# Adding the expert gates into a zeroed DRAM scratch by indexed accumulating transfers, head by head, in place of one-hot products

## The chip, the cores and the metric

The kernel runs on one core of a Trainium2 chip. The metric is the device time of one execution in microseconds. PE is the matrix engine, DVE is VectorE, ACT is ScalarE, POOL is GpSimd; "PEld" is PE's weight load. SP issues the weight stream. A "q" behind a name is the engine's queue for DMA issues.

## What is computed

Two transformer blocks on 256 tokens of width 2048 in float32. The part that matters is the expert layer of the first block (`peer`):

```python
q = (t @ wq).reshape(T, 8, 2, 128)
s1 = einsum('thd,hnd->thn', q[:, :, 0], k1)      # 128 key scores per head and half
s2 = einsum('thd,hnd->thn', q[:, :, 1], k2)
v1, i1 = top_k(s1, 16)
v2, i2 = top_k(s2, 16)
cand = v1[..., :, None] + v2[..., None, :]       # 256 pairs
sc, pos = top_k(cand.reshape(T, 8, 256), 16)
idx = ...                                         # i1 * 128 + i2 of the 16 best pairs
g = softmax(sc)
act = gelu(einsum('thkd,td->thk', u[idx], t))
out = einsum('thk,thkd->td', g * act, v[idx])
```

There are 128 x 128 = 16384 experts; a token picks 8 heads x 16 of them.

## The kernel before

**How the layer is made dense.** For the first G = 48 tokens the kernel gathers the rows of the picked experts. For the other TD = 208 tokens it computes all experts: in eight rounds r, each of 2048 experts, a product u_r (16 feature units), gelu, a multiplication by the gates, and a product e_r (16 units). The gates of a token are a 128 x 128 matrix (second key by first key), zero but for the picked pairs, where they hold the sum of the softmax values. A round needs the gates of 16 first keys; they lie in DRAM (`gates_d`) and come in four loads of four first keys into `gbuf` (`load_gates(r, g)`, on POOL's queue).

**The weight stream.** Every product takes its weights from one stream of 1 MB units. SP loads unit k into `raw[k % 4]`. ACT writes its rounded high part into `split` (`hi`, line 713), DVE the rest (`lo`, line 1163), and PE multiplies high and low parts: 48 matmuls of 208 columns in a unit of u0 or u1 (lines 1996 to 1998). `ahead(u)` on ACT and DVE prepares the unit three behind u; from `NEAR0` on it is two behind, with the low part in `split` too, so that the load of the next unit need not wait for PE. The order of the stream around the change is wq (16 units), u0, u1, e0, e1, u2, e2 and so on.

**The order around the change, as written out by hand.** During wq, PE adds the key scores of head h in step `KEYS_AT`, ACT copies them to `s_sb`, and DVE searches the best 16 in two passes of eight (`best8`, lines 1515 to 1522: maximum, its index, its replacement), first of four key rows and then, after `sums` (line 1537), of two rows of pairs. Searches of two heads are interleaved, and a split (`ahead`, `fill`) stands between the pieces. This reaches into u0. Then, for all heads at once, DVE turns positions into keys (`differ`, lines 1586 and 1593), ACT takes the exponentials between u0's units, DVE divides by the sums. Picks lie in `picked`, transposed by PE into `pickT`.

**The gates in u1.** Tokens go in 52 groups of four. For each, DVE writes a one-hot tile of the second keys (`pick_b`, line 1619) and four of the first keys times the gate (`pick_a`, line 1624), PE multiplies them (`gate_group`, line 2341) at up to five places inside a u1 unit, ACT copies the bank to `stage` (line 950), and after four groups ACT's queue writes 1 MB to `gates_d` (line 954). The gates of the first eight first keys also go to `gbuf` directly (line 957). POOL meanwhile issues 36 small DMAs for the gathered tokens' indices, gates and scales (lines 628 to 630).

**Behind it.** DVE multiplies u0's result `act0` by the gates and splits it for e0 in four groups `gated0(g)` (lines 1642, 1654, 1657). e0's first unit needs all 16 tiles. During e0 DVE alternates `accumulate(0, k)`, `ahead` and `gated1(k)`, which does the same for u1's result and e1. Later rounds use `gate_hidden`. The gathers for the first 48 tokens (line 639, 96 of them) start behind e0.

Of the kernel before, what the change touches and what calls it, by code (L numbers as in the profile page):

```python
# [15 lines left out]
F32 = mybir.dt.float32  # L16
# [25 lines left out]
TBLOCK, TBLOCKS = 16, TD // 16  # L42
# [40 lines left out]
for _name, _n in [("ident", P), ("tri", P), ("ones", P), ("ntri", P), ("gt", P), ("flip", P),  # L83
                  ("mask", 2 * P), ("iota", P), ("sel", G)]:
    CONSTS[_name] = (_c, _c + _n)
    _c += _n
# [41 lines left out]
def build(nc, x_in, mem_in, stream, cols_in, consts_in, rows_in, wide_in, wdtf_in, keys_in,  # L128
          rel_in, onehot_in, u_rows, v_rows, out):
    ctx = ExitStack()  # L130
    with ctx:
# [89 lines left out]
        cand = at("cand", [P, 2, TT, 256], F32, work_at + 24576)  # L221
        differ = at("differ", [P, PICKS, TOPK], U32, work_at + 24576)
        pick_a = at("pick_a", [P, 8, P], F32, work_at + 24576)
        pick_b = at("pick_b", [P, 8, P], F32, work_at + 28672)
        gbuf = at("gbuf", [P, 4, TBLOCKS, 4 * TBLOCK], F32, work_at + 16384)
        pk = work_at + 32768

        top_v = [at(f"top_v{tt}", [P, 16, TOPK], F32, o) for tt, o in enumerate((pk, wdtf_at))]
        top_i = [at(f"top_i{tt}", [P, 16, TOPK], U32, o + 1024) for tt, o in enumerate((pk, wdtf_at))]
        top_x = at("top_x", [P, 16, TOPK], U32, pk + 2048)  # L230
        sc = at("sc", [P, TT, PEER_HEADS, TOPK], F32, pk + 3072)
        pos = [at(f"pos{tt}", [P, PEER_HEADS, TOPK], U32, pk + o) for tt, o in enumerate((4096, 12928))]
        posab = at("posab", [P, 2, PICKS], U32, pk + 4608)
        slot_x = at("slot_x", [P, TOPK], U32, pk + 5632)
        picked = at("picked", [P, TT, 3, PICKS], F32, pk + 6656)
        pickT = at("pickT", [P, 3, T], F32, pk + 9728)
        gsum = at("gsum", [P, TT, PEER_HEADS], F32, pk + 12800)
        first = at("first", [P, PEER_HEADS], F32, pk + 12864)
# [3 lines left out]
        stage = at("stage", [P, 2, PEER_KEYS, TBLOCK], F32, a2_at + 16384)  # L242
# [24 lines left out]
        rows_at = work_at + 16384 + 4 * TBLOCKS * 4 * TBLOCK * 4  # L267
# [89 lines left out]
        picks_done = sem("picks_done")  # L357
        pickT_psum = sem("pickT_psum")
        oha_done = sem("oha_done")
        ohb_done = sem("ohb_done")  # L360
        g_mm = sem("g_mm")
        g_evict = sem("g_evict")
        g_write = [sem(f"g_write{i}") for i in range(2)]
        g_early = sem("g_early")
# [46 lines left out]
        gates_d = nc.dram_tensor("gates_scratch", (TBLOCKS, P, PEER_KEYS * TBLOCK), F32, kind="Internal").ap()  # L411
# [43 lines left out]
        NEAR0, NEAR1 = UNIT0["u1"], UNIT0["ck"]  # L455
# [66 lines left out]
        KEYS_AT = {2 * h + 3: h for h in range(PEER_HEADS)}  # L522
        WQ_STEPS = 18
# [45 lines left out]
        def _(pool):  # L569
# [2129 lines left out]
```

## Time and profile before

| | us |
|---|---|
| median of 3 runs | 3057.14 (3055.29 to 3058.13) |
| profiled execution, first to last instruction | 3054.2 |
| PE busy in it | 3004.1 (98%) |
| DVE busy | 2268.2 (74%) |
| ACT busy | 1409.3 (46%) |
| POOL busy | 186.1 (6%) |

The profiled execution is given by its span of 3054.2 us alone; a time of that one execution that includes what lies around the span is not listed. The median of the runs is 2.9 us above the span. A busy share is a mean over stages with different limits, so the stages around the change are read by themselves below.

### The profile page before, as it was taken

How to read it: one execution, taken by the hardware profiler on the slowest of the kernel's cores; microseconds unless marked ns; L12 is line 12 of the kernel's file. 1: busy time of each engine (PE TensorE's matmuls, PEld its weight loads, DVE VectorE, ACT ScalarE, POOL GpSimd, SP SyncE). 2: the span in 40 equal slices, each digit the busy share in tenths (PEclk: the TensorE clock that was granted, in tenths of full speed). 3: DMA queues.
4: the chain of work that ended last, by engine and by line, in shares of the span. 5: the costliest groups of instructions: out<-in, count | busy, mean ns of one | idle time of the engine just before them, and what ended most of it. 6: DMA issues, size and time to landing. Idle time of an engine off the chain costs nothing.

```text
span 3054.2 us, 49503 instructions
## 1 busy us (share of the span) xinstructions
PE 3004.1 (98%) x19430; PEld 2799.9 (92%) x19430; DVE 2268.2 (74%) x3252; ACT 1409.3 (46%) x1718; POOL 186.1 (6%) x233
## 2 busy tenths in 40 slices
PE   8999999999999999999999999999999999999998
PEld 8899889999999999999999999999788888888887
DVE  5777559999768988888888877698656646555564
ACT  4464443466445454545454456434445333333333
POOL 1000000020001111111111000000000000000000
PEclk9999999999999999999999999999999999999999
DMA  5443454466668999999999874544444555555554
GB/s 209 178 139 138 157 205 173 166 234 231 237 252 313 358 352 356 351 349 343 359 342 350 317 280 166 194 166 161 157 172 167 185 192 190 191 183 191 192 186 159
DMA packets 102147, 705.59 MB, mean 231 GB/s; under 512 B 13016, under 2 KB 13040, under 8 KB 18464
## 3 DMA queue, kind: packets, MB, share of 16 engines
q1 hardware_dynamic: 78272, 562.07, 50.5%
q0 software_dynamic: 21872, 128.10, 11.9%
q10 hardware_dynamic: 1872, 13.63, 1.1%
q8 instruction: 87, 1.43, 0.2%
q14 instruction: 44, 0.36, 0.0%
HBM read 685.46 MB, written 18.24 MB: 230 GB/s over the span
## 4 chain that ended last, share of the span: by engine, by line
PE 87%; DVE 9%; ACT 2%; issue 1%; DMA 1%; SPq 0%; POOL 0%; POOLq 0%; ACTq 0%; DVEq 0%
PE bank L2018 29%; PE bank L2019 15%; PE bank L2048 7%; PE bank L2050 7%; PE bank L2049 7%; PE bank L1996 6%; PE bank L1997 6%; PE bank L1998 6%; PE bank L2024 2%; DVE raw_lo L1163 2%; DVE split L1163 1%; DVE pick_a L1624 1%; ACT split L713 1%; PE bank L2115 1%; DVE pick_b L1619 1%
## 5 line engine op out<-in xcount | busy, mean ns | idle before, releaser
L2018 PE MATMUL bank<-a_both,split 128*128 128x416 f32 (+1 forms) x3840 | 1222.5, 376 | 2.3 <-DVE split L1163 1.9
L1163 DVE TENSOR_TENSOR raw_lo<-raw,split 128x2048 fp32r<-128x2048 f32 x292 | 668.6, 2290 | 390.2 <-ACT split L713 387.1
L713 ACT ACTIVATE split<-raw 128x2048 fp32r<-128x2048 f32 x308 | 588.6, 1911 | 487.8 <-DMA raw<-stream_dram 308.1
L2018 PEld LDWEIGHTS bank<-a_both,split 128*128 128x128 f32 x3840 | 721.1, 188 | 55.8 <-issue 5.9
L2019 PE MATMUL bank<-a_both,split 128*128 128x208 f32 x3072 | 762.0, 258 | 0.0
L2019 PEld LDWEIGHTS bank<-a_both,split 128*128 128x128 f32 x3072 | 584.6, 190 | 0.9
L1996 PE MATMUL bank<-a_both,split 128*128 128x256 f32 (+1 forms) x1984 | 572.5, 289 | 12.0 <-DVE raw_lo L1163 6.8
L1163 DVE TENSOR_TENSOR split<-raw,split 128x2048 fp32r<-128x2048 f32 x240 | 549.6, 2290 | 33.0 <-ACT split L713 11.0
L729 ACT ACTIVATE split<-raw 128x1536 fp32r<-128x1536 f32 x224 | 333.8, 1490 | 505.3 <-PE bank L2019 501.3
L1997 PE MATMUL bank<-a_both,split 128*128 128x256 f32 (+1 forms) x1984 | 560.4, 282 | 0.0
L1998 PE MATMUL bank<-a_both,raw_lo 128*128 128x256 f32 (+1 forms) x1728 | 488.8, 283 | 0.0
L1996 PEld LDWEIGHTS bank<-a_both,split 128*128 128x128 f32 x1984 | 384.2, 194 | 17.6 <-issue 9.8
L1997 PEld LDWEIGHTS bank<-a_both,split 128*128 128x128 f32 x1984 | 384.3, 194 | 0.6
L2048 PE MATMUL bank<-split,a_both 128*128 128x512 f32 x952 | 374.4, 393 | 1.5 <-DVE a_both L1176 1.5
L2050 PE MATMUL bank<-split,a_both 128*128 128x512 f32 x952 | 370.7, 389 | 0.0
L2049 PE MATMUL bank<-raw_lo,a_both 128*128 128x512 f32 x952 | 370.5, 389 | 0.0
L1998 PEld LDWEIGHTS bank<-a_both,raw_lo 128*128 128x128 f32 x1728 | 333.5, 193 | 0.0
L2019 PE MATMUL bank<-a_both,raw_lo 128*128 128x256 f32 x1024 | 277.2, 281 | 0.0
L2048 PEld LDWEIGHTS bank<-split,a_both 128*128 128x128 f32 x952 | 178.8, 188 | 39.4 <-DVE a_both L1176 2.2
L2050 PEld LDWEIGHTS bank<-split,a_both 128*128 128x128 f32 x952 | 178.7, 188 | 37.4
L2049 PEld LDWEIGHTS bank<-raw_lo,a_both 128*128 128x128 f32 x952 | 178.9, 188 | 36.2
L2019 PEld LDWEIGHTS bank<-a_both,raw_lo 128*128 128x128 f32 x1024 | 193.3, 189 | 6.3
(344 smaller groups left out, 3071.0 us busy)
## 6 DMA issues: line engine op xcount, KB each, us to landing
raw<-stream_dram SPq DMA_DIRECT2D x532, 1024.0 KB
gates_scratch<-stage ACTq DMA_DIRECT2D x13, 1024.0 KB, 4.3
gbuf<-gates_scratch POOLq DMA_DIRECT2D x30, 416.0 KB, 6.9
x<-x_dram SPq DMA_DIRECT2D x4, 512.0 KB, 7.1
x_scratch<-x POOLq DMA_DIRECT2D x1, 2048.0 KB, 11.4
mem<-mem_dram POOLq DMA_DIRECT2D x1, 2048.0 KB, 9.5
xm<-x_scratch POOLq DMA_DIRECT2D x1, 2048.0 KB, 12.1
out_dram<-x SPq DMA_DIRECT2D x4, 512.0 KB, 3.0
```

The costliest lines, as they stand in the source:

```text
L713: eng.activation(high(k, is_near(k))[:, :], raw[:, k % RAW, :], ACT.Copy).then_inc(hi_done, 1)
L729: eng.activation(high(k, is_near(k))[:, 0:PART], raw[:, k % RAW, 0:PART], ACT.Copy)
L1163: eng.tensor_tensor(low(k, is_near(k)), raw[:, k % RAW, :], high(k, is_near(k))[:, :].bitcast(F32), ALU.subtract).then_inc(split_done, 1)
L1996: mm(o, hi[:, ks], tile(0, kt), start=kt == 0, stop=False)
L1997: mm(o, hi[:, ks], tile(1, kt), start=False, stop=False)
L1998: last = mm(o, lo[:, ks], tile(0, kt), start=False, stop=kt == KT - 1)
L2018: mm(o, hi[:, ks], pair, start=kt == 0, stop=False)
L2019: inst = mm(o2, lo[:, ks], pair[:, 0, :], start=False, stop=False, skip_group_check=True)
L2024: mm(o, hi[:, ks], pair, start=False, stop=True).then_inc(mm_done, 1)
L2048: mm(o, tile(0, k0 + k)[:, ts], hi[:, ns], start=first and k == 0, stop=False)
L2049: mm(o, tile(0, k0 + k)[:, ts], lo[:, ns], start=False, stop=False)
L2050: last = mm(o, tile(1, k0 + k)[:, ts], hi[:, ns], start=False, stop=end and k == 3)
```

## The change

The gates are no longer built by products. During v1 and z, POOL writes zeros over all of `gates_d`, now laid out as one row of 128 x 208 values for each second key. DVE works head by head: search, positions to keys for this head, offsets of its 16 picks (second key x `GATE_ROW` + first key x 208 + token), and gates, with the splits for the weights distributed by a table (`SPLIT_BEHIND`) over six places per head. ACT takes the exponentials per head. When a head is ready, POOL issues 16 indexed DMAs for the upper 128 tokens and 16 for the 80 tokens below them (after a small DMA that moves these 80 to partition 0). Each adds one pick of all its tokens, single values of 4 bytes, to `gates_d`. The adds of a head wait for those of the previous head with the same tokens. After the last has landed, POOL loads the gates of round 0, and only then issues the 36 small DMAs. The one-hot tiles, their products, their copies and their writes go, u1 runs three units ahead like u0 (`NEAR0` moves to e0), and the key scores stand inside the units.

```diff
-TBLOCK, TBLOCKS = 16, TD // 16
+GATE_ROW = PEER_KEYS * TD
+FAR = P - G
...
-        gates_d = nc.dram_tensor("gates_scratch", (TBLOCKS, P, PEER_KEYS * TBLOCK), F32, kind="Internal").ap()
+        gates_d = nc.dram_tensor("gates_scratch", (P * GATE_ROW, 1), F32, kind="Internal").ap()
+        gates_rows = gates_d.rearrange("(p n) one -> p (n one)", p=P)
...
-        GROUPS = TD // 4
-        GATES_AFTER = (2, 5, 8, 11, 15)
-        GATES_UNIT = {(q + 2) // 5: [n for n in range(GROUPS) if (n + 2) // 5 == (q + 2) // 5] for q in range(GROUPS)}
-
-        LAST_GROUP = max(GATES_UNIT)
+        SPLIT_BEHIND = {}
+        _k = 3
+        for _h, _counts in enumerate([(1, 1, 1, 0, 2, 0), (1, 0, 1, 1, 1, 0), (1, 0, 1, 1, 1, 0), (1, 1, 1, 0, 1, 1),
+                                      (1, 1, 1, 0, 2, 0), (1, 1, 1, 1, 1, 0), (1, 1, 1, 1, 1, 0), (2, 1, 1, 0, 2, 0)]):
+            for _piece, _n in enumerate(_counts):
+                if (_h, _piece) == (0, 0):
+                    _k += 1
+                SPLIT_BEHIND[_h, _piece] = [_k + i for i in range(_n)]
+                _k += _n
+        PICK_UNITS = 48
+        ZERO_PARTS = GATE_ROW // 2048
+        assert GATE_ROW == ZERO_PARTS * 2048
+        EXP_AFTER = {SPLIT_BEHIND[h, 4][0] - 3: h for h in range(PEER_HEADS)}
...
-        NEAR0, NEAR1 = UNIT0["u1"], UNIT0["ck"]
+        NEAR0, NEAR1 = UNIT0["e0"], UNIT0["ck"]
...
-        KEYS_AT = {2 * h + 3: h for h in range(PEER_HEADS)}
-        WQ_STEPS = 18
+        KEYS_AT = {2 * h + 2: h for h in range(PEER_HEADS)}
+        KEYS_KT = 4
...
+            eng.wait_ge(wd_done, 2)
+            eng.memset(zeros[:, :], 0.0).then_inc(zeros_set, 1)
+            eng.wait_ge(zeros_set, 1)
...
+                if h == 8:
+                    for n in range(ZERO_PARTS):
+                        eng.wait_ge(mm_done, UNIT0["v1"] + n + 1)
+                        cs = slice(n * 2048, n * 2048 + 2048)
+                        eng.dma_start(gates_rows[:, cs].rearrange("p (a b) -> p a b", b=256),
+                                      zeros[:, :].unsqueeze(1).to_broadcast([P, 8, 256])).then_inc(s_zeros, 16)
...
+            def add_picks(tt, h):
+
+                if h > 0:
+                    eng.wait_ge(s_added[tt], 16 * TOPK * h)
+                for k in range(TOPK):
+                    if tt == 1:
+                        c = TOPK * h + k
+                        idx, src = offs[:, 1, 0, c:c + 1], offs[:, 1, 1, c:c + 1].bitcast(F32)
+                    else:
+                        idx, src = near_offs[0:FAR, h, 0, k:k + 1], near_offs[0:FAR, h, 1, k:k + 1].bitcast(F32)
+                    eng.indirect_dma_start(gates_d, bass.IndirectOffsetOnAxis(ap=idx, axis=0), src, None,
+                                           compute_op=ALU.add).then_inc(s_added[tt], 16)
+
+            eng.wait_ge(s_zeros, 16 * ZERO_PARTS)
+            for h in range(PEER_HEADS):
+                eng.wait_ge(picks_ready, h + 1)
+                eng.dma_start(near_offs[0:FAR, h, :, :], offs[G:P, 0, :, TOPK * h:TOPK * h + TOPK]).then_inc(s_near, 16)
+                add_picks(1, h)
+                eng.wait_ge(s_near, 16 * (h + 1))
+                add_picks(0, h)
+
+            def load_gates(r, g):
+                at0 = (16 * r + 4 * g) * TD
+                eng.dma_start(gbuf[:, g, :], gates_rows[:, at0:at0 + 4 * TD]).then_inc(g_full[g], 16)
+
+            def gather(n):
+
+                src = u_rows if n < GJ else v_rows
+                eng.indirect_dma_start(got[:, n % 2, :], None, src,
+                                       bass.IndirectOffsetOnAxis(ap=row_idx[:, n % GJ:n % GJ + 1], axis=0))\
+                    .then_inc(s_got[n % 2], 16)
+
+            for tt in range(TT):
+                eng.wait_ge(s_added[tt], 16 * PICKS)
+            for g in range(4):
+                load_gates(0, g)
...
+            def gate_exp(h):
+
+                eng.wait_ge(sm_dve, h + 1)
+                for tt in range(TT):
+                    eng.activation(sc[:, tt, h, :], sc[:, tt, h, :], ACT.Exp, bias=nfirst[:, h, tt:tt + 1],
+                                   accum_out=gsum[:, h, tt:tt + 1]).then_inc(sm_act, 1)
+
+            for s in range(PICK_UNITS):
...
+                elif s < 32:
+                    if s == 16:
+                        eng.wait_ge(s_xw, 16)
+                    eng.activation(act0[:, s - 16, 0:TD], bank[s % 4][:, 0:TD], ACT.Gelu).then_inc(bank_free, 1)
+                else:
+                    eng.activation(act1[:, s - 32, 0:TD], bank[s % 4][:, 0:TD], ACT.Gelu).then_inc(bank_free, 1)
+                ahead(UNIT0["wq"] + s)
+                if s in EXP_AFTER:
+                    gate_exp(EXP_AFTER[s])
...
+            def split_behind(h, piece):
+                for k in SPLIT_BEHIND[h, piece]:
+                    ahead(UNIT0["wq"] + k - 3)
+
+            def slots_of(h):
+
+                hs = slice(TOPK * h, TOPK * h + TOPK)
+                eng.tensor_scalar(nfirst[:, h, :], sc[:, :, h, 0], -1.0, None, ALU.mult).then_inc(sm_dve, 1)
+                own.did(eng.tensor_tensor(key_x[:, :, :, :], top_i[:, :, 2 * h:2 * h + 2, :],
+                                          slot_x[:, :].unsqueeze(1).unsqueeze(1).to_broadcast([P, TT, 2, TOPK]), ALU.bitwise_or))
+                own.did(eng.tensor_scalar(posab[:, 0, :, :], pos[:, :, h, :], 4, 7, ALU.logical_shift_right, ALU.logical_shift_left))
+                own.did(eng.tensor_scalar(posab[:, 1, :, :], pos[:, :, h, :], 15, 7, ALU.bitwise_and, ALU.logical_shift_left))
+                own.wait()
+                for half in range(2):
+                    own.did(eng.tensor_tensor(differ[:, half, :, :, :],
+                                              posab[:, half, :, :].unsqueeze(3).to_broadcast([P, TT, TOPK, TOPK]),
+                                              key_x[:, :, half, :].unsqueeze(2).to_broadcast([P, TT, TOPK, TOPK]),
+                                              ALU.bitwise_xor))
+                own.wait()
+                for half in range(2):
+                    own.did(eng.tensor_reduce(key_at[:, half, :, hs], differ[:, half, :, :, :], AX.X, ALU.min))
+                own.wait()
+                own.do(eng.scalar_tensor_tensor(row_off[:, :, :], key_at[:, 0, :, hs], float(TD),
+                                                C("tok").unsqueeze(2).to_broadcast([P, TT, TOPK]), ALU.mult, ALU.add))
+                own.do(eng.scalar_tensor_tensor(offs[:, :, 0, hs], key_at[:, 1, :, hs], float(GATE_ROW), row_off[:, :, :],
+                                                ALU.mult, ALU.add))
+
+            def gates_for(h):
+
+                hs = slice(TOPK * h, TOPK * h + TOPK)
+                eng.wait_ge(sm_act, TT * (h + 1))
+                own.do(eng.reciprocal(gsum[:, h, :], gsum[:, h, :]))
+                eng.tensor_tensor(offs[:, :, 1, hs].bitcast(F32), sc[:, :, h, :],
+                                  gsum[:, h, :].unsqueeze(2).to_broadcast([P, TT, TOPK]), ALU.mult).then_inc(picks_ready, 1)
...
+            for h in range(PEER_HEADS):
+                eng.wait_ge(sk_copied, TT * (h + 1))
+                best8(0, key_rows(h))
+                split_behind(h, 0)
+                best8(1, key_rows(h))
+                split_behind(h, 1)
+                sums(h)
+                best8(0, pair_rows(h))
+                split_behind(h, 2)
+                best8(1, pair_rows(h))
+                split_behind(h, 3)
+                slots_of(h)
+                split_behind(h, 4)
+                gates_for(h)
+                split_behind(h, 5)
...
-                if g >= 2:
-                    eng.wait_ge(g_full[g], 16)
+                eng.wait_ge(g_full[g], 16)
...
-                if k == 0:
-                    eng.wait_ge(s_idx, 16 * 3 * SET_DMAS)
                 if k % 4 == 0:
-                    eng.wait_ge(g_full[k // 4], 16 * (1 + (k >= 8)))
+                    eng.wait_ge(g_full[k // 4], 32)
...
-            eng.wait_ge(g_early, TBLOCKS)
+            ahead(u1 + 14)
             gated0(0)
-            for k in range(LAST_GROUP, 16):
-                ahead(u1 + k)
-                if k == LAST_GROUP:
-                    gated0(1)
-                if k in (LAST_GROUP + 1, LAST_GROUP + 2):
-                    gated0(k - LAST_GROUP + 1)
+            gated0(1)
+            ahead(u1 + 15)
+            gated0(2)
+            gated0(3)
...
-            def gate_group(q):
-
-                eng.wait_ge(ohb_done, q + 1)
-                if q >= 4:
-                    eng.wait_ge(g_evict, q - 3)
-                for i in range(4):
-                    eng.wait_ge(oha_done, 4 * q + i + 1)
-                    j = 4 * (q % 2) + i
-                    mm(bank[4 + q % 4][:, i * P:i * P + P], pick_b[:, j, :], pick_a[:, j, :], start=True, stop=True)\
-                        .then_inc(g_mm, 1)
...
+            for s in range(16):
+                eng.wait_ge(split_done, UNIT0["wq"] + s + 1)
+                eng.wait_ge(bank_free, 4 * ROUND0["wq"] + s + 1)
+                feature_unit(s, a1, "ln2" if s == 0 else None, rest_turn if s == 0 else keys_inside if s in KEYS_AT else None)
+            for s in range(16, 20):
+                eng.wait_ge(split_done, UNIT0["wq"] + s + 1)
+                eng.wait_ge(bank_free, 4 * ROUND0["wq"] + s + 1)
+                feature_unit(s, a1, between=keys_inside if s in KEYS_AT else None, c0=G)
+            feature("u0", 12, a1, first=4, c0=G)
+            feature("u1", 16, a1, c0=G)
```

## Rows read from the trace of the kernel before

**Rows 1.** The page: its span, the busy time of each engine, the DMA share in 40 slices

```profile
span 3054.2 us, 49503 instructions
...
PE 3004.1 (98%) x19430; PEld 2799.9 (92%) x19430; DVE 2268.2 (74%) x3252; ACT 1409.3 (46%) x1718; POOL 186.1 (6%) x233
...
DMA  5443454466668999999999874544444555555554
```

**Rows 2.** Windows: stretch, its length, busy us of each engine, granted clock, DMA share, GB/s

```profile
531.00:626.00 95.00, 89.35 (x766) 88.66 (x764) 88.06 (x196) 37.94 (x38) 0.55 (x2) 0.96 0.47 172
626.00:772.00 146.00, 138.51 (x1190) 136.71 (x1187) 133.84 (x326) 90.71 (x97) 24.01 (x41) 0.98 0.67 235
772.00:854.00 82.00, 82.00 (x548) 81.47 (x547) 66.18 (x98) 35.74 (x36) 4.58 (x4) 1.00 0.68 235
```

**Rows 3.** Timeline of ACT, wq to u1: start, us, engine, line, operation [idle before]

```profile
466.24 0.38 ACT L927 ACTIVATE qT<-bank 128x256 f32<-128x256 f32 x1 [3.92 <-PE bank L1998]
...
528.26 0.38 ACT L927 ACTIVATE qT<-bank 128x256 f32<-128x256 f32 x1 [3.91 <-PE bank L1998]
...
577.37 0.34 ACT L932 ACTIVATE act<-bank 128x208 f32<-128x208 f32 x1 [3.21 <-PE bank L1998]
...
582.73 0.34 ACT L932 ACTIVATE act<-bank 128x208 f32<-128x208 f32 x1 [3.21 <-PE bank L1998]
...
718.26 0.34 ACT L966 ACTIVATE act<-bank 128x208 f32<-128x208 f32 x1 [0.25 <-PE bank L1998]
...
728.60 0.34 ACT L966 ACTIVATE act<-bank 128x208 f32<-128x208 f32 x1 [0.24 <-PE bank L1998]
...
771.90 0.34 ACT L966 ACTIVATE act<-bank 128x208 f32<-128x208 f32 x1 [3.22 <-PE bank L1998]
```

**Rows 4.** Groups by line, 630 to 740 us: busy us, mean ns

```profile
L1624 DVE TENSOR_SCALAR pick_a<-consts,pickT 128x128 f32<-128x128 f32 x203 | 56.7, 346 | 0.0
L2341 PE MATMUL bank<-pick_a,pick_b 128*128 128x128 f32 x410 | 56.0, 279 | 4.4 <-DVE pick_a L1624 2.9 <-ACT stage L950 1.5
```

**Rows 5.** Timeline of DVE in u0

```profile
548.09 2.29 DVE L1163 TENSOR_TENSOR raw_lo<-raw,split 128x2048 fp32r<-128x2048 f32 x1
...
562.31 2.29 DVE L1163 TENSOR_TENSOR raw_lo<-raw,split 128x2048 fp32r<-128x2048 f32 x1
...
583.21 2.29 DVE L1586 TENSOR_TENSOR differ<-posab,top_x 128x2048 uint32<-128x2048 uint32 x1
```

**Rows 6.** Timeline of POOL: the first two gathers, and a later one

```profile
854.19 1.07 POOL L639 DMA_INDIRECT got<-u_rows_dram,row_idx  x1 [0.31 <-issue]
855.57 2.02 POOL L639 DMA_INDIRECT got<-u_rows_dram,row_idx  x1 [0.30 <-issue]
...
1077.87 0.93 POOL L639 DMA_INDIRECT got<-u_rows_dram,row_idx  x1 [8.68 <-DVE row_dot L1719]
```

**Rows 7.** Timeline of DVE at the same two places

```profile
854.45 2.29 DVE L1163 TENSOR_TENSOR split<-raw,split 128x2048 fp32r<-128x2048 f32 x1
...
1077.85 2.34 DVE L1163 TENSOR_TENSOR split<-raw,split 128x2048 fp32r<-128x2048 f32 x1
```

**Rows 8.** Groups by line on POOL, whole span: busy us, mean ns, idle before

```profile
L639 POOL DMA_INDIRECT got<-v_rows_dram,row_idx x48 | 45.3, 943 | 330.5 <-DVE set_rows L1724 308.4 <-DVE row_dot L1719 12.5 <-DVE set_rows L1721 9.6
...
L628 POOL DMA_DIRECT2D row_idx<-pick_idx x12 | 5.9, 493 | 170.8 <-DVE pick_idx L1607 170.8
```

**Rows 9.** DMA issues: queue, count, KB each, median us from issue to landing

```profile
gates_scratch<-stage ACTq DMA_DIRECT2D x13, 1024.0 KB, 4.3
gbuf<-gates_scratch POOLq DMA_DIRECT2D x30, 416.0 KB, 6.9
...
row_idx<-pick_idx POOLq DMA_DIRECT2D x8, 1.0 KB, 3.5
...
rel_scratch<-relT POOLq DMA_DIRECT2D x1, 16.0 KB, 2.2
```

**Rows 10.** Timeline of DVE, one group of `gated0`

```profile
747.19 1.22 DVE L1642 TENSOR_TENSOR act<-act,gbuf 128x208 f32<-128x208 f32 x4
748.33 0.79 DVE L1654 CAST e_both<-act 128x208 fp32r<-128x208 f32 x4
```

More of the change, by code:

```diff
@@ L229, in build @@
[L229 to L235, printed above, removed]
@@ L356, in build @@
         sm_act = sem("sm_act")
[L357 to L364, printed above, removed]
+        picks_ready = sem("picks_ready")
+        s_zeros = sem("s_zeros")
+        zeros_set = sem("zeros_set")
+        s_near = sem("s_near")
+        s_added = [sem(f"s_added{i}") for i in range(TT)]
         g_full = [sem(f"g_full{i}") for i in range(4)]
@@ L916, in _ @@
                     ahead(UNIT0["out1"] + 15)
-            for s in range(WQ_STEPS):
+            def gate_exp(h):
[4 more added lines that the diff above has]
+            for s in range(PICK_UNITS):
                 if s in KEYS_AT:
@@ L1594, in _ @@
-            for tt in range(TT):
-                eng.wait_ge(sm_act, tt + 1)
-                own.do(eng.tensor_reduce(gsum[:, tt, :], sc[:, tt, :, :], AX.X, ALU.add))
-                own.do(eng.reciprocal(gsum[:, tt, :], gsum[:, tt, :]))
-                eng.tensor_tensor(picked[:, tt, 2, :].rearrange("p (h k) -> p h k", h=PEER_HEADS), sc[:, tt, :, :],
-                                  gsum[:, tt, :].unsqueeze(2).to_broadcast([P, PEER_HEADS, TOPK]), ALU.mult)\
-                    .then_inc(picks_done, 1)
@@ L1640, in weigh @@
+            eng.wait_ge(picks_ready, PEER_HEADS)
+            own.did(eng.scalar_tensor_tensor(pick_idx[:, :], key_at[0:G, 0, 0, :], float(PEER_KEYS), key_at[0:G, 1, 0, :],
+                                             ALU.mult, ALU.add))
+            own.wait()
+            eng.tensor_copy(pick_f[:, :], offs[0:G, 0, 1, :].bitcast(F32)).then_inc(idx_done, 1)
+            for k in range(SPLIT_BEHIND[PEER_HEADS - 1, 4][-1] + 1, PICK_UNITS):
+                ahead(UNIT0["wq"] + k - 3)
             def weigh(tile, g, j):
-                eng.tensor_tensor(blocks(tile), blocks(tile), gates_of(g, j), ALU.mult).then_inc(g_used, 1)
+                eng.tensor_tensor(tile, tile, gbuf[:, g, j * TD:j * TD + TD], ALU.mult).then_inc(g_used, 1)
@@ L2344, in _, with key_scores @@
-            for k in range(16):
-                groups = GATES_UNIT.get(k, [])
-                places = GATES_AFTER if k else GATES_AFTER[-len(groups):]
-                def between(kt, groups=groups, places=places):
-                    if kt in places and places.index(kt) < len(groups):
-                        gate_group(groups[places.index(kt)])
-                eng.wait_ge(split_done, UNIT0["u1"] + k + 1)
-                eng.wait_ge(bank_free, 4 * ROUND0["u1"] + k + 1)
-                if k == 0:
-                    picks_turn()
-                feature_unit(k, a1, between=between, c0=G, near=True)
+            def key_scores(h):
+                if h == 0:
+                    eng.wait_ge(s_keys, 16)
+                if h >= 4:
+                    eng.wait_ge(sk_copied, TT * (h - 3))
+                eng.wait_ge(bank_free, 4 * ROUND0["wq"] + 4 + 2 * h + 2)
+                for tt in range(TT):
+                    for n in (2 * h, 2 * h + 1):
+                        c = tt * T + (n % 2) * P
+                        last = mm(bank[4 + h % 4][:, c:c + P], qT[:, n, tt * P:tt * P + P], keys[:, n, :],
+                                  start=True, stop=True)
+                last.then_inc(sk_done, 1)
```

200 lines of the change are left out of this document (36 added, 164 removed).

## The prediction

> **What bounds the kernel now.** I read the page first. The span is 3054.2 us and PE is busy for 98% of it [rows 1], so only stretches in which PE does something other than weight units, or waits, can give time back. The table by windows finds them: PE idles 5.6 us in 531 to 626 and 7.5 us in 626 to 772 [rows 2]. The second stretch hides more than its idle time, so I went to the timeline of ScalarE, where each evacuation marks the end of a weight unit. A u0 unit takes 582.73 - 577.37 = 5.36 us; a u1 unit with its five gate groups takes 728.60 - 718.26 = 10.34 us [rows 3]. From the end of wq (528.26) to the end of u1 (771.90) there are 243.6 us for 32 units, and 32 x 5.36 is 171.5 [rows 3]. So 72.1 us of this stretch are the price of the old gates: the gate products on PE and the one-hot tiles for them on VectorE [rows 4], and stalls. Behind it, in e0 and later, PE shows no idle time that depends on the gates' making. The question is thus when e0 can begin: now at 771.90.
>
> **What is removed.** 52 groups of four one-hot products, their VectorE tiles, ScalarE's 52 evacuations and 13 writes. If nothing replaced them as a bound, u1 would end 72.1 us earlier, less 0.9 us for head 7's four key products, which move from wq into the first u0 unit (an estimate from the products of the same shape in the old groups: records of 279 ns [rows 4], which overlap): 528.26 + 0.9 + 171.5 = 700.7. This is the ceiling: 71 us.
>
> **VectorE's new order.** In the steady state one head's search (both halves of the key rows and of the pairs, and the sums) lies between the splits at 548.09 and 562.31, with two splits in it: 14.2 - 2 x 2.2 = 9.8 us [rows 5]; in four separate pieces, with their own waits, 10.0. The slots: now 2048 elements take 2.29 us [rows 5]; a head has two xors and two reductions of 512, 4 x 0.57 = 2.3, and some ten small instructions, by estimate 1.9 with the gates' two. Sum 14.2 us, eight heads 114 us. The 39 splits between them at 2.25 are 88 us. 202 us from 445 on would be 647, but the splits may not run ahead: the one behind the last head's slots waits for unit 39 of the 48, which ends near 700.7 - 8 x 5.36 = 658. So the last picks are ready near 660 and VectorE has some ten us to spare; the exponentials, two table loads and two short activations per head, lie behind ScalarE's 2.2 us per unit. I cost all this at nothing; if the cover were gone, a unit would be late by the few us by which a head overruns five units. The first picks: head 0's rows are there at about 445, 14.2 us of work and five splits (11.3) later it is 470.5; its last split needs wq's sixth unit, done at 466.24 [rows 3], 1.9 of ScalarE and 2.3 of VectorE, the same 471.
>
> **POOL's new work, and the bound.** 256 indexed adds (8 heads x 16 picks x 2 token tiles; half with 128 indices, half with 80), and eight small plain DMAs, all on POOL's queue in order, from 471 on. e0's gates are loaded only when the last has landed. No add is in the trace. The nearest rows are the indexed gathers: 128 indices, mean 943 ns for the later 48 [rows 8]. Two things in the trace speak for more. First, the one pair of gathers issued back to back has a gap of 0.30 us between them that is put down to issue [rows 6]; an add every 0.94 + 0.30 = 1.24 us. Second, the second of this pair took 2.02 us instead of 0.94. It began at 855.57, inside a VectorE split (two operands in SBUF) from 854.45 to 856.74 [rows 7]: it ended 0.85 us after the split did, as if it had waited for the split's end to read its indices and then done its work. The gather at 1077.87 started 0.02 us after a split and lost nothing, and that split took 2.34 in place of 2.29 [rows 6, 7]: the read is short, and whoever is first goes first. I take both as real. The Trainium skill, SBUF - State Buffer, section "Who interferes with whom", states this as a rule: a VectorE instruction with two SBUF inputs contends with a GpSimd instruction that reads SBUF, and the later one waits. The trace agrees with it in that one pair (2.02 against 0.94 us); by the rule the sum is the likeliest one below, without it the gap-only one.
>
> The price of an add in the steady state: 1.24 us for 128 indices. A plain small DMA is 0.49 us [rows 8], so indices cost about 0.45 us per 128 and an 80-index add about 1.24 - 0.17 = 1.07. Lower bound for both 0.77 and 0.94 (no gap); an accumulating one may cost more than a gather, upper bound see the rivals. Work: 128 x 1.24 + 128 x 1.07 + 8 x 0.49 = 300 us.
>
> Held time: each split of 2.29 us stops POOL once its running add is through (on average half of 1.16, 0.6 us, into it): 1.7 us lost per 5.36 us unit. From 471 to 700.7 that is 229.7 / 5.36 = 42.9 splits, 73 us; xors, sums and small two-input instructions about 0.9 per head, 7 us. POOL gets 229.7 - 80 = 150 us of its 300 done by the end of u1. PE then has nothing to do, the splits stop, and POOL needs another 150 us: the last add is issued at 851.
>
> **The tail after the last add.** Landing about 3 us (16 KB to DRAM took 2.2, a write of 1 MB 4.3); the first gate load 6.9 us [rows 9]. VectorE's four groups of 1.22 + 0.79 + 1.23 [rows 10] and a split, 15.5 us, then feed e0's first unit, which needs all 16 tiles; 3 + 6.9 + 15.5 = 25.4, less the 4.8 us that the unit takes anyway, 21. The 36 small row DMAs (0.49 each, 17.7 us [rows 8]) now stand between these loads and those for e1's gates, on which VectorE waits in its first gated1 with e0's fourth split behind it: e0's loads end by 3 + 4.7, the row DMAs by 25.4, the next load lands at 32.3, and PE, fed with three units, loses about 3 us. Together 24 us: e0 begins in effect at 851 + 24 = 875, not at 771.9, **+103 us**. Behind that, the gate loads are of longer rows but stay hidden: in 772 to 854 PE was busy all of it.
>
> Other moves at nothing: the 13 writes of zeros (1 MB each) follow the first 13 units behind v1's start, in the second to third slice of the page; their cover is the DMA engines' idle share, five to six tenths there [rows 1], and without it each such unit would be late by up to 3 us. u1 now refills its weights later, as u0 does today without a wait for DMA. The index and score tiles in x's place wait for a write long landed.
>
> **Rivals.**
> - *Held, but no gap* (adds of 0.94 and 0.77, 223 to 245 us of work, 1.8 lost per split): 143 us done by 700.7, the last issued at 781 to 803, e0 in effect at 805 to 827: +33 to +55, taken as +44. For it: the gap may be the start of a lone pair; against: it is the only pair.
> - *Gap, but not held* (300 us of work from 471): 771 + 24 = 795, +23. For it: the later 48 gathers, 943 ns on average [rows 8], show no hold at all; against: each of them follows the end of a VectorE job, so none began inside a long two-input instruction.
> - *Faster: POOL keeps pace.* Neither gap nor hold, adds as the lone gather. 223 to 245 us from 471: the last at 694 to 716, e0 at 718 to 740: -54 to -32, taken as -40. It decides below (771.9 - 24 - 471 - 4) / 256 = 1.07 us per add, all waits included. For it: heads are ready every 26.8 us (five units) and 32 such adds take 28 to 31 us, nearly a match.
> - *DMA engines are the bound.* If each add had to land before the next goes on, at 2.2 us [rows 9]: 256 x 2.2 = 563, the last landed at 1034, e0 at 1055: +283. Against: 36 small DMAs issued every 0.49 us landed with a median of 3.5 us and no growing delay [rows 8, 9], though into SBUF. The Trainium skill, DMA: Bandwidth & Descriptors, section "Anatomy of one DMA", puts about 2 us on a single software DMA, most of it the receipt from memory; here that would give a sum of 512 us if nothing overlapped, and no run here shows an add yet.
>
> **The numbers.** Durations come from one execution with a span of 3054.2 us; the median of the three runs is 3057.14, 2.9 more, which I keep as a constant outside the span. Likeliest: 3057 + 103 = 3160, chance 0.38 (own range 3125 to 3200 from the 80-index price and the small losses). Held, no gap, 3101: 0.17. Gap only, 3080: 0.10. Faster, 3017: 0.22. DMA-bound, up to 3340: 0.10. Within 0.2% (6 us, about what a measurement of this kernel can tell from no change): 0.03. Range 3010 to 3230: it takes in the faster case but for its best end and leaves out most of the DMA-bound one. Faster 0.22, same 0.03, slower 0.75.
>
> **What the changed profile would show.** The adds as 256 indexed DMAs on POOL with a mean near 1.7 us while splits run and near 0.94 with 0.3 us gaps after u1; u0 and u1 units of 5.36 us; PE idle from about 700 for some 150 us, with the granted clock at its lower level around it, and its wait put down to VectorE's gated tiles and these to the gate loads. I am wrong if adds shorter than 1.07 us follow each other under the splits, if VectorE's splits grow late instead (u0 and u1 units above 5.4 us), or if the adds are issued on time but land late.

## The result and the profile after

The changed kernel takes 3298.64 us (median of 4 runs, 3295.86 to 3300.15) against 3057.64 us for the kernel before in the same session: ratio 1.0784, 95% interval 1.0769 to 1.0799. It is slower by 241 us; 3160 was forecast, with a range up to 3230.

The page of the changed kernel: the span, busy time of each engine, three rows of slices, and the chain that ended last, by engine and by line. They answer to [rows 1].

```profile
span 3293.8 us, 48665 instructions
...
PE 2953.6 (90%) x19008; PEld 2750.2 (83%) x19008; DVE 2195.6 (67%) x3062; ACT 1366.0 (41%) x1689; POOL 625.1 (19%) x513
...
POOL 1100028888883011111111110000000000000000
PEclk9999999975558999999999999999999999999999
DMA  5853456652215789999999997454444555555554
...
PE 76%; POOL 13%; DVE 4%; issue 3%; ACT 2%; DMA 1%; SPq 0%; POOLq 0%; DVEq 0%; ACTq 0%
PE bank L1989 26%; PE bank L1990 13%; POOL gates_scratch L649 13%; PE bank L2019 6%; PE bank L2021 6%; PE bank L2020 6%; PE bank L1967 4%; PE bank L1968 4%; PE bank L1969 4%; PE bank L1995 2%; DVE raw_lo L1173 1%; DMA raw<-stream_dram 1%; PE bank L2086 1%; DVE split L1173 1%; ACT split L749 1%
```

POOL is busy for only 19% of the span, yet one line of it, L649, the adds, holds 13% of the chain. The busy shares alone would not have pointed there. The table by windows shows the stretch (columns as in [rows 2]):

```profile
531.00:626.00 95.00, 95.00 (x854) 95.00 (x852) 86.43 (x224) 48.78 (x56) 82.81 (x43) 1.00 0.66 199
626.00:700.00 74.00, 74.00 (x665) 74.00 (x664) 46.47 (x89) 34.87 (x39) 65.16 (x31) 1.00 0.66 195
700.00:800.00 100.00, 1.76 (x16) 1.58 (x15) 0.98 (x1) 2.14 (x2) 83.25 (x58) 0.52 0.26 24
800.00:900.00 100.00, 0.00 (x0) 0.00 (x0) 0.00 (x0) 0.00 (x0) 83.24 (x58) 0.50 0.20 0
900.00:1000.00 100.00, 2.54 (x8) 2.13 (x8) 5.22 (x21) 0.00 (x0) 83.17 (x68) 0.50 0.23 18
1000.00:1030.00 30.00, 26.46 (x141) 25.35 (x142) 24.18 (x50) 8.13 (x8) 14.54 (x29) 0.77 0.56 198
1030.00:1100.00 70.00, 70.00 (x468) 69.55 (x467) 55.67 (x85) 30.09 (x30) 6.09 (x6) 1.00 0.72 257
```

Until 700 us the change does what it should: PE is busy all of 531 to 700. Then three hundred us follow in which nothing but POOL works, at 83% busy. The rest of its time is gaps. The DMA engines are 0.20 busy in the middle of it, so there is no shortage of transfer capacity.

ScalarE's timeline at the end of u1, to set beside [rows 3]:

```profile
680.36 0.34 ACT L976 ACTIVATE act<-bank 128x208 f32<-128x208 f32 x1 [3.21 <-PE bank L1969]
...
685.72 0.34 ACT L976 ACTIVATE act<-bank 128x208 f32<-128x208 f32 x1 [3.21 <-PE bank L1969]
...
701.79 0.34 ACT L976 ACTIVATE act<-bank 128x208 f32<-128x208 f32 x1 [3.21 <-PE bank L1969]
```

A u1 unit takes 5.36 us instead of 10.34 in [rows 3], and u1 ends at 701.79 where 771.90 stood. The row at 701.79 is the evacuation of u1's last unit.

The adds among the instructions that touch `gates_scratch`, by operation: durations in ns (shortest, median, longest), first and last start in us; then what ended the idle time before them:

```profile
L649 POOL DMA_INDIRECT gates_scratch<-offs x128: 1539/1548/3647, 473.8 to 960.5; - x128
L649 POOL DMA_INDIRECT gates_scratch<-near_offs x128: 1406/1412/3335, 508.8 to 988.1; - x128
...
  issue: 78.0, 256
...
  DMA gates_scratch<-near_offs: 1.6, 1
```

Most of the answer lies in these two lines. An undisturbed add takes 1.55 us with 128 indices and 1.41 with 80, and in front of each of the 256 stands a gap of 78.0 / 256 = 0.30 us. After the last of them POOL waits 1.6 us for all to have landed.

POOL's timeline around one held add and at the end, then VectorE's at the first place:

```profile
579.46 1.55 POOL L649 DMA_INDIRECT gates_scratch<-offs  x1 [0.30 <-issue]
581.32 3.60 POOL L649 DMA_INDIRECT gates_scratch<-offs  x1 [0.30 <-issue]
585.23 1.42 POOL L649 DMA_INDIRECT gates_scratch<-near_offs  x1 [0.30 <-issue]
...
988.12 1.41 POOL L649 DMA_INDIRECT gates_scratch<-near_offs  x1 [0.30 <-issue]
991.12 2.26 POOL L662 DMA_DIRECT2D gbuf<-gates_scratch  x4 [1.59 <-DMA gates_scratch<-near_offs]
```

```profile
581.20 2.29 DVE L1173 TENSOR_TENSOR raw_lo<-raw,split 128x2048 fp32r<-128x2048 f32 x1
583.41 0.87 DVE L1525 MAX8 top_v<-s_sb 128x8 f32<-128x128 f32 x4
```

The add at 581.32 begins 0.12 us into a split that runs to 583.49, 2.17 us later, and takes 3.60 - 1.55 = 2.05 us more than the one before it. The add at 585.23, which begins beside a search, loses nothing.

Over the whole trace (a sum over all adds, not shown row by row): 40 splits begin between 472.8 and 701.8, and 39 adds begin inside one of them and are longer for it. Each loses the rest of that split less 0.07 to 0.13 us, together 53 us, 1.36 us on average. Three more adds begin within 0.03 us of a split's start and lose at most 0.03 us. Of the other holds, one `differ` instruction costs 0.45 us, and nothing else costs as much. All adds together are 54 us longer than undisturbed ones.

The very first add shows what an add costs when nothing is queued before it:

```profile
473.78 1.72 POOL L649 DMA_INDIRECT gates_scratch<-offs  x1 [0.31 <-issue]
```

It is no shorter than the later ones. So the 1.55 us are not a wait for transfers of earlier adds.

The waits that this becomes, total us, times, longest:

```profile
PE bank L1989 <- DVE e_both L1632: 299.2, 4, 295.5
DVE act L1620 <- DMA gbuf<-gates_scratch: 295.6, 2, 293.7
```

One wait of 295.5 us on PE, of 293.7 on VectorE, both behind POOL's last add.

### The profile page after: what moved, and what is told of

It is laid out like the page before. It is cut to its first block, busy times and chain, and to the rows that moved or that the text cites. A ratio compares the mean times of both kernels' runs of the same rounds, so it can differ in the third digit from the quotient of the medians.

```text
span 3293.8 us, 48665 instructions
## 1 busy us (share of the span) xinstructions
PE 2953.6 (90%) x19008; PEld 2750.2 (83%) x19008; DVE 2195.6 (67%) x3062; ACT 1366.0 (41%) x1689; POOL 625.1 (19%) x513
## 4 chain that ended last, share of the span: by engine, by line
PE 76%; POOL 13%; DVE 4%; issue 3%; ACT 2%; DMA 1%; SPq 0%; POOLq 0%; DVEq 0%; ACTq 0%
PE bank L1989 26%; PE bank L1990 13%; POOL gates_scratch L649 13%; PE bank L2019 6%; PE bank L2021 6%; PE bank L2020 6%; PE bank L1967 4%; PE bank L1968 4%; PE bank L1969 4%; PE bank L1995 2%; DVE raw_lo L1173 1%; DMA raw<-stream_dram 1%; PE bank L2086 1%; DVE split L1173 1%; ACT split L749 1%
## 5 line engine op out<-in xcount | busy, mean ns | idle before, releaser
L1173 DVE TENSOR_TENSOR raw_lo<-raw,split 128x2048 fp32r<-128x2048 f32 x308 | 705.5, 2291 | 402.8 <-ACT split L749 399.6
L1969 PE MATMUL bank<-a_both,raw_lo 128*128 128x256 f32 (+1 forms) x1984 | 557.7, 281 | 0.0
L1173 DVE TENSOR_TENSOR split<-raw,split 128x2048 fp32r<-128x2048 f32 x224 | 513.0, 2290 | 30.3 <-ACT split L749 8.4
L1989 PE MATMUL bank<-e_both,split 128*128 128x416 f32 x480 | 151.7, 377 | 299.2 <-DVE e_both L1632 299.2
L1969 PEld LDWEIGHTS bank<-a_both,raw_lo 128*128 128x128 f32 x1984 | 381.2, 192 | 0.0
L1989 PEld LDWEIGHTS bank<-e_both,split 128*128 128x128 f32 x480 | 92.9, 194 | 301.9 <-issue 295.6
L649 POOL DMA_INDIRECT gates_scratch<-offs x128 | 230.3, 1799 | 39.0 <-issue 39.0
L2019 PEld LDWEIGHTS bank<-split,a_both 128*128 128x128 f32 x952 | 178.7, 188 | 39.2 <-DVE a_both L1186 2.2
```

The lines of the kernel that those rows point to most:

```text
L649: eng.indirect_dma_start(gates_d, bass.IndirectOffsetOnAxis(ap=idx, axis=0), src, None, compute_op=ALU.add).then_inc(s_added[tt], 16)
L1173: eng.tensor_tensor(low(k, is_near(k)), raw[:, k % RAW, :], high(k, is_near(k))[:, :].bitcast(F32), ALU.subtract).then_inc(split_done, 1)
L1969: last = mm(o, lo[:, ks], tile(0, kt), start=False, stop=kt == KT - 1)
L1989: mm(o, hi[:, ks], pair, start=kt == 0, stop=False)
L2019: mm(o, tile(0, k0 + k)[:, ts], hi[:, ns], start=first and k == 0, stop=False)
```

## The experiments

All kernels below start from the changed one. The ratios compare with the kernel before on the same chip; its median was 3057.40 us beside experiments 1 to 4 and 3058.41 beside 5 and 6. The differences from the changed kernel are between sessions, and these medians (3057.64 beside the changed kernel) say how well that can be done: to about 1 us.

**1. Take the accumulation away.** The adds become plain indexed writes, so that a pair chosen by several heads keeps one gate only.

```diff
-                    eng.indirect_dma_start(gates_d, bass.IndirectOffsetOnAxis(ap=idx, axis=0), src, None,
-                                           compute_op=ALU.add).then_inc(s_added[tt], 16)
+                    eng.indirect_dma_start(gates_d, bass.IndirectOffsetOnAxis(ap=idx, axis=0), src, None).then_inc(s_added[tt], 16)
```

> The changed kernel with the 256 indexed DMAs as plain writes instead of accumulating ones (so the gates are the last write, not the sum: part of the computation is left out). An indexed gather from DRAM took 0.94 us of POOL before, an accumulating one takes 1.55 (128 indices) and 1.41 (80). Theory A, the accumulation costs the 0.6 us: plain writes take about 0.94 and 0.81, the issue gap of 0.30 stays; work 128 x 1.24 + 128 x 1.11 + 8 = 309 us, some 75 us held by splits before u1 ends, last one issued near 857, time about 3165. Theory B, it is the direction or the 4-byte elements that cost it: 1.55 and 1.41 stay, time 3299 as the changed kernel.

Measured: 3166.73 us, ratio 1.0359 (1.0338 to 1.0380), 132 us less than the changed kernel. The same two rows of this kernel, and three of its POOL timeline:

```profile
L649 POOL DMA_INDIRECT gates_scratch<-offs x128: 954/958/2962, 476.2 to 840.3; - x128
L649 POOL DMA_INDIRECT gates_scratch<-near_offs x128: 898/905/2898, 502.9 to 859.7; - x128
```

```profile
704.41 0.96 POOL L649 DMA_INDIRECT gates_scratch<-offs  x1 [0.30 <-issue]
705.67 0.96 POOL L649 DMA_INDIRECT gates_scratch<-offs  x1 [0.30 <-issue]
706.94 0.96 POOL L649 DMA_INDIRECT gates_scratch<-offs  x1 [0.30 <-issue]
```

A plain indexed write costs what a gather costs (0.96 against the 0.94 of [rows 8]), and the gap of 0.30 us stays. So the accumulation is 1.55 - 0.96 = 0.59 us and 1.41 - 0.905 = 0.51 us of POOL's own time per DMA: 128 x 0.59 + 128 x 0.51 = 141 us, of which 132 came back. The shorter writes run into more of VectorE's instructions: held time, summed over the trace, is 63 us here for 54 in the changed kernel. The first write takes 1.08 us where the first add took 1.72, so the surcharge is there with nothing queued. What POOL does in this time no run shows.

That this kernel lands near the forecast, 3167 for 3160, is in part luck. Its work is 128 x 1.26 + 128 x 1.205 + 8 = 324 us where I had 300, and its held time is 63 where I had 80; the two errors nearly cancel.

**2 and 3. Fewer adds.** Only 8, or only 4, of the 16 picks of each head and token tile are added; the rest of the gates is left out. The waits that count the adds count fewer of them. VectorE's order and everything else stay.

```diff
+ADDED = 8
...
-                for k in range(TOPK):
+                for k in range(ADDED):
```

In the second kernel `ADDED` is 4.

> The changed kernel with 8 of the 16 picks of each head added (128 DMAs instead of 256; the other half of the gates is left out). Theory A, POOL's time per DMA sets e0's start: work 64 x 1.85 + 64 x 1.71 + 8 = 236 us from 473, about 54 us held, the last issued near 763, e0 in effect 22 us later at 785, time near 3070. Theory B, the DMA engines' side sets it, at a rate that the changed kernel hides behind POOL: the last add lands well behind its issue, and the wait of POOL for it is more than the 1.6 us of the changed kernel.

> The changed kernel with 4 of the 16 picks of each head added (64 DMAs; three quarters of the gates are left out). Theory A: a head's adds (4 x 1.85 + 4 x 1.71 + 1, and up to 9 us held) take less than the 26.8 us between heads, so POOL waits for picks, the last are ready near 675, e0 begins about when u1 ends plus what is left of the 22 us tail, near 712: time near 2998, the most that this order could give if adds cost nothing. Theory B, the new order of VectorE's work loses time by itself that POOL now hides: well above 3000.

Measured: 3065.25 us with 8 (ratio 1.0027, 1.0016 to 1.0038), 3003.8 with 4 (0.9827, 0.9810 to 0.9843). From 256 to 128 adds the time falls by 233.4 us, 1.82 us per add; from there to 64 by 61.4, 0.96 each. With 8 picks, the 80-index adds and POOL's wait for the last landing:

```profile
L650 POOL DMA_INDIRECT gates_scratch<-near_offs x64: 1406/1415/3518, 493.2 to 760.3; - x64
...
  DMA gates_scratch<-near_offs: 1.7, 1
```

The last add starts at 760.3, where POOL's own time puts it (near 763 was expected), and the wait for landing is 1.7 us against 1.6 with twice the adds: nothing piles up on the DMA engines' side.

The slope breaks because with 64 adds POOL keeps pace. Its waits and its timeline in the kernel with 4 picks:

```profile
POOL near_offs L656 <- DVE offs L1585: 100.2, 8, 33.1
```

```profile
666.20 0.70 POOL L656 DMA_DIRECT2D near_offs<-offs  x1 [13.74 <-DVE offs L1585]
667.19 1.60 POOL L650 DMA_INDIRECT gates_scratch<-offs  x1 [0.30 <-issue]
...
684.85 3.35 POOL L650 DMA_INDIRECT gates_scratch<-near_offs  x1 [0.30 <-issue]
...
692.37 2.26 POOL L663 DMA_DIRECT2D gbuf<-gates_scratch  x4 [4.17 <-DMA gates_scratch<-near_offs]
```

POOL now waits 100.2 us for picks, and the last head's are there at 666.2 (I had 660 in the prediction and 675 before this run). The add behind the pause of 13.74 us still takes 1.60 us: an idle stretch makes it no cheaper. The other side of the change thus stands alone here: without the old gates and with VectorE's new order, 53.6 us can be had of the 71 that I called the ceiling. Most of the rest is the tail, whose loads begin at 692 and which ends with e0's first unit at 719.5. By the slope of the first step I estimate that the kernel would break even at 128 - 7.8 / 1.82, about 124 of the 256 adds; no run tries it.

**4. Take the hold away.** In the last 26 units before e0 the VectorE split takes its second operand from PSUM (a bank of other data); its duration stays 2.29 us.

```diff
+                if isinstance(k, int) and UNIT0["wq"] + 22 <= k < UNIT0["e0"]:
...
+                    eng.tensor_tensor(parts(low(k, False)), parts(raw[:, k % RAW, :]),
+                                      bank[5][:, :].unsqueeze(1).to_broadcast([P, 4, 512]), ALU.subtract).then_inc(split_done, 1)
```

> The changed kernel with all its adds, but VectorE's low-part subtraction takes its second operand from PSUM instead of SBUF in the last 26 units before e0 (so those low parts hold other values; same number of instructions and elements). Theory A, an add's start waits for a running VectorE instruction with two SBUF operands: from about 551 us on no add is longer than 1.56 or 1.43 us, the 40 us that adds were held there come back, time near 3259. Theory B, adds are held by any long VectorE instruction, or by ScalarE's or the weights' traffic at the same time: durations up to 3.6 us stay, time 3299.

Measured: 3260.87 us, ratio 1.0667 (1.0646 to 1.0689), 38 us less than the changed kernel. VectorE and POOL of this kernel, at one of the new splits:

```profile
601.25 2.29 DVE L1175 TENSOR_TENSOR raw_lo<-raw,bank 128x2048 fp32r<-128x2048 f32 x1 [1.38 <-ACT split L749]
```

```profile
600.31 1.41 POOL L649 DMA_INDIRECT gates_scratch<-near_offs  x1 [0.30 <-issue]
602.02 1.41 POOL L649 DMA_INDIRECT gates_scratch<-near_offs  x1 [0.30 <-issue]
603.73 1.41 POOL L649 DMA_INDIRECT gates_scratch<-near_offs  x1 [0.30 <-issue]
```

The add at 602.02 begins and ends inside a VectorE instruction of the same shape and length and takes its plain 1.41 us. It is no exception: 32 adds begin inside one of the new splits, and none takes more than 0.06 us over the undisturbed duration. Held time over the trace falls from 54 to 16 us, which is the 38 us of the measured time; what is left belongs to the splits before the edited ones, to one of e0's (0.90 us) and to small two-input instructions. So a busy VectorE does not hold an add. The split's second operand does, when it lies in SBUF.

The Trainium skill, SBUF - State Buffer, section "Who interferes with whom", says that VectorE's second port pair is GpSimd's own, that this pair is locked for one of them at a time, and that a VectorE instruction with at most one SBUF input does not contend (outside certain modes). Both runs agree: 3.60 against 1.55 us beside a split with two SBUF operands, 1.41 beside one with a PSUM operand.

The hold does not catch every DMA that POOL issues. In the changed kernel, a split in the tail and one of POOL's plain row DMAs beside it:

```profile
1000.95 2.29 DVE L1173 TENSOR_TENSOR split<-raw,split 128x2048 fp32r<-128x2048 f32 x1
```

```profile
1001.79 0.48 POOL L680 DMA_DIRECT2D row_idx<-pick_idx  x1
```

The plain DMA takes the 0.48 us of its neighbours. Among POOL's DMAs here, the held ones are those with indices, which lie in SBUF; that the reading of them is what waits is my inference.

**5. Is the price per DMA or per index?** The adds of the first token tile take 16 indices instead of 80.

```diff
-                        idx, src = near_offs[0:FAR, h, 0, k:k + 1], near_offs[0:FAR, h, 1, k:k + 1].bitcast(F32)
+                        idx, src = near_offs[0:16, h, 0, k:k + 1], near_offs[0:16, h, 1, k:k + 1].bitcast(F32)
```

> The 128 adds of the first token tile take 16 indices each instead of 80 (the gates of 64 tokens are left out); everything else is as in the changed kernel. Theory A (an accumulating DMA costs POOL a fixed time, and an index almost nothing): the two durations of the changed kernel, 1.55 us with 128 indices and 1.41 us with 80, give 0.0029 us per index and 1.18 us without any; a 16-index add takes 1.22 to 1.24 us with the same gap of 0.30 us, the 128 of them save 128 x 0.18 = 23 us, and the time is about 3276 us. Rival B (the accumulation is paid per element, so that the fixed part is that of a plain indexed write and the 0.6 us more belong to the elements): the add falls by a good part of 0.6 us more, to 0.8 us or less, 78 us or more are saved, and the time is 3220 us or less.

Measured: 3283.22 us, ratio 1.0734 (1.0713 to 1.0756), 15 us less than the changed kernel. In this kernel:

```profile
L649 POOL DMA_INDIRECT gates_scratch<-near_offs x128: 1282/1289/3399, 510.0 to 973.7; - x128
```

1.29 us for 16 indices, 1.41 for 80, 1.55 for 128: a fifth of the indices costs 91% of the time. Theory A is right in kind and off in size: the line through the two larger ones (1.22 to 1.24) lies too low, and 128 x 0.12 = 15 us came instead of 23. Rival B wanted 0.8 us or less and falls. Most of the price belongs to the instruction, not to its elements. How much of the accumulation's own 0.51 to 0.59 us is fixed stays open, since no plain write of 16 indices was run. An add of 16 still costs 0.38 us more than a plain write of 80; if a plain write of 16 is no dearer than one of 80, at least 0.38 of the 0.51 us remain at a fifth of the indices.

**6. The small row DMAs in the tail.** POOL issues the four gate loads for e1 ahead of the 36 row DMAs.

```diff
+            for g in range(4):
+                eng.wait_ge(g_used, 4 * (g + 1))
+                load_gates(1, g)
             eng.wait_ge(idx_done, 1)
...
-            for r in range(1, 3):
+            for r in range(2, 3):
```

> POOL issues the four gate loads for e1 before the 36 small row DMAs instead of behind them; nothing is left out. Theory: the row DMAs hold the first of these loads until 1012.39 us and VectorE's first tile of the next unit until 1016.15, which made the second unit of e0 take 6.15 us where the others take 4.8; with the loads ahead that unit is 4.8 to 5.0 us, and the time falls by 1.4 us, to about 3297 us. Rival: the row DMAs cost the 5 us by which the whole kernel lost more than e0's start was late (239.6 against 234.6 us), and the time falls to about 3294 us; or the row DMAs, now behind the loads, are late for the gathers, and it rises.

Measured: 3300.32 us (4 runs, 3293.24 to 3301.05), ratio 1.0791 (1.0773 to 1.0809): no change that can be told. The median supports neither 3297 nor 3294, but with runs 8 us apart the 1.4 us of the theory could not have been seen in it. The trace decides: the second unit of e0 was to take 4.8 to 5.0 us, and it did not. In the changed kernel the second unit of e0 does show the wait; this is VectorE there:

```profile
1012.02 2.28 DVE L1173 TENSOR_TENSOR split<-raw,split 128x2048 fp32r<-128x2048 f32 x1
1016.15 0.37 DVE L1620 TENSOR_TENSOR act<-act,gbuf 128x208 f32<-128x208 f32 x1 [1.85 <-DMA gbuf<-gates_scratch]
```

and this is VectorE with the loads ahead, followed by one window of it:

```profile
1012.48 2.28 DVE L1176 TENSOR_TENSOR split<-raw,split 128x2048 fp32r<-128x2048 f32 x1
1014.68 0.37 DVE L1623 TENSOR_TENSOR act<-act,gbuf 128x208 f32<-128x208 f32 x1
...
1018.50 2.29 DVE L1176 TENSOR_TENSOR split<-raw,split 128x2048 fp32r<-128x2048 f32 x1
...
1023.29 2.29 DVE L1176 TENSOR_TENSOR split<-raw,split 128x2048 fp32r<-128x2048 f32 x1
```

```profile
1012.00:1018.00 6.00, 6.00 (x36) 5.93 (x35) 3.98 (x7) 1.94 (x3) 6.00 (x13) 0.83 0.35 104
```

The wait is gone, and the unit still takes 1018.50 - 1012.48 = 6.02 us against 4.79 for the next. PE is busy all of it at a granted clock of 0.83, and 6.0 x 0.83 is 5.0: after some 295 idle us it has come back at its lower level (0.50, which is 1.2 GHz) and is only now let up. In the changed kernel PE is busy in all of these 6 us as well, with the same 0.83. The gates' wait lay beside that slower PE.

## Why the prediction was wrong, point by point

**The step that failed is a term of the sum that was mis-sized: "1.24 us for 128 indices" and "about 1.24 - 0.17 = 1.07" for an 80-index add.** With the gap they are 1.55 + 0.30 = 1.85 and 1.41 + 0.30 = 1.71. I took the duration of a gather for that of an accumulating write and left the surcharge without an upper bound ("an accumulating one may cost more than a gather, upper bound see the rivals"). The only rival there that could hold it was the one bound by the DMA engines, and its mechanism is another. Experiment 1 shows the surcharge: 0.59 and 0.51 us of POOL's time per DMA. The 300 us of work were 128 x 1.85 + 128 x 1.71 + 8, about 464. Of the 164 us between them, 141 are the accumulation. Another 17 are a second wrong price: I took indices to cost 0.45 us per 128, from the difference of an indexed and a plain DMA, and so gave an 80-index DMA 0.77 us; the plain write of experiment 1 takes 0.905, and 48 indices fewer save only 0.05 us. Of the rest, 4 are the small DMAs, which cost 1 us each with their gap, where I had 0.49.

The miss of the last add's time, in my own terms:

- *First picks at 471*: 472.8. ScalarE's rows show 1.1 us of this already lost before 200 us. +2.
- *Work of 300 us*: 464. +164.
- *Held time of 80 us*: 53. -27. The mechanism was right (experiment 4). The size was not. There were 40 splits and not 42.9: wq's units take 6.2 us and not 5.36 (from 466.24 to 528.26 are ten of them [rows 3]), and the splits for u1 are through before u1 is. Each hold cost 1.36 us on average and not 1.7: an add already running is spared, and the real one runs longer than mine. The xors and sums, for which I had 7 us, cost about 1. In experiment 1, with shorter DMAs, held time is 63 us. So the underpriced add made the hold look dearer than it is, and this error partly undid the other.
- *Last add issued at 851*: these sum to 990; it was through at 989.5.
- *Tail of 24 us*: e0's first unit ended at 1011.32 where it had ended at 776.71 (the two rows below), 234.6 us later. So e0 was in effect begun at 771.9 + 234.6 = 1006.5, 17 us behind the last add. -7. Landing took 1.6 us and the first load 3.6, where I had 3 and 6.9, and the 3 us for the row DMAs did not come. The 6.9 is the median of 30 loads beside the weight stream, which kept the DMA engines 0.68 busy in 772 to 854 [rows 2]; in 900 to 1000 they are at 0.23. In the kernel with 4 picks, where the weight stream runs beside it, the landing took 4.2.
- *"PE, fed with three units, loses about 3 us"* by the row DMAs: experiment 6 says nothing that can be measured; the slower clock covers it.

VectorE's first evacuation in e0, before and in the changed kernel:

```profile
776.71 0.38 DVE L1679 COPY accT<-bank 128x208 f32<-128x208 f32 x1 [0.34 <-PE bank L2024]
```

```profile
1011.32 0.38 DVE L1652 COPY accT<-bank 128x208 f32<-128x208 f32 x1 [1.85 <-PE bank L1995]
```

2 + 164 - 27 - 7 = 132, and 103 + 132 = 235, which is e0's shift. Another 5 us are lost behind it: 1.3 in e0's second unit, the rest in small pieces up to the end, which I did not trace.

**What held.** u1's end: from wq's end at 529.39 it took 172.4 us, the 0.9 + 171.5 of the prediction to the tenth; 701.8 for 700.7. VectorE's new order costed at nothing: PE was busy all of 531 to 700 and units stayed at 5.36, and experiment 3 shows 53.6 us of gain once POOL is out of the way. Zero writes at nothing: ScalarE's rows were 0.4 us later before them and 1.1 behind, so they cost at most 0.7 us. The gap of 0.30 us, read off one pair in [rows 6], stood in front of all 256. So did the hold, read off one instruction of 2.02 us in [rows 6, 7].

**The rivals.** *Held, but no gap* and *gap, but not held* each drop a mechanism that the trace shows. *POOL keeps pace* decided below 1.07 us per add, all waits included; they took 517 / 256 = 2.02. Its condition is met in experiment 3 alone, with a quarter of the adds. *DMA engines are the bound* gave 3340, which is nearest to the time that came, and is nevertheless wrong: the wait for landing is 1.6 us after the last of 256, the engines are 0.2 busy, the first add takes as long as the rest, and removing the accumulation shortened the instruction on POOL, not a wait. (The 3.5 us that I set against this rival is the median of the eight `row_idx` DMAs in [rows 9], not of all 36.) The Trainium skill, DMA: Bandwidth & Descriptors, section "Anatomy of one DMA", which I had cited beside this rival, counts its 2 us mostly as the receipt from memory and calls the making of descriptors small. The landing is of that order (a wait of 1.6 us, once, at the end). The second half does not describe these DMAs if POOL's busy time is that making: it is 0.96 us for a plain indexed write and 1.55 with the addition. The trace shows the busy time, not what is done in it. A rival that gives about the right time is not thereby the cause.

## What to carry to other kernels

Count indirect DMAs as instructions of the engine that issues them: here 1.6 to 1.85 us each with the accumulation and the gap, for 16 to 128 indices, in series, with the DMA engines at 0.2. The 256 of them are about 460 us of one engine, and a design that wants them must either have that long before the result is needed or have fewer of them (here under half). When an operation is missing from the trace, bound it from above by a number even if the nearest row is of a simpler kind, and ask of each modifier (here the addition) on which engine it costs time; I had only allowed that it may cost more. A lone pair of instructions in a trace can be enough for a mechanism, if the numbers on both engines fit to a tenth of a us.

## What was not expected of the hardware

- The accumulation costs the issuing engine, not only the transfer: 1.55 against 0.96 us (128 indices), 1.41 against 0.905 (80), with nothing else changed.
- An add barely depends on its number of indices: 1.29, 1.41 and 1.55 us for 16, 80 and 128.
- A held add loses nearly exactly the rest of the VectorE instruction: at 581.32 it was 2.05 us more, with 2.17 us of the split to go, and 39 adds follow this within 0.06 us. A split whose second operand is in PSUM holds nothing (at most 0.06 us in 32 adds), and a plain DMA issued under a split is not held (0.48 us).
- PE's clock after some 295 us without work: PE starts again at 997.21 and works with pauses; in 1006 to 1012 the granted clock was still 0.50, in 1012 to 1018 it was 0.83, from 1018 on 1.00. By experiment 6 the second unit took 6.0 us instead of the 4.8 of the next one, 1.2 us.
